# A decoder step with product-key retrieval: the normed rows h2 move from SBUF into two banks of PSUM, and the two score components take turns in the other two

## The chip, the cores and the metric

The kernel runs on one core of one Trainium2 chip. The metric is the device time of one execution in microseconds (us), the median over several runs. Lower is better.

## The reference, cut to what matters

One layer of a decoder: norm, one input projection, differential attention (4 heads, two components a head) beside a pooling mixer, one output projection, a residual, and then PEER: each token picks 16 experts for each of 8 heads out of 16,384, takes the dot of its normed row with each expert's row of `w_u`, and adds up the experts' rows of `w_v`, weighted by the gelu of the dot and a gate. 1,040 prompt rows (16 of them meta tokens) and 32 sample rows go through it.

```python
def diff_attn(q, k, v, q_pos, k_pos, lam):
    s = jnp.einsum('bqhcd,bkhcd->bchqk', q, k) * (QK_DIM ** -0.5)
    s = jnp.where(k_pos[None, :] <= q_pos[:, None], s, NEG)
    p = jax.nn.softmax(s, axis=-1)
    a = p[:, 0] - lam * p[:, 1]
    return jnp.einsum('bhqk,bkhd->bqhd', a, v)

def peer(xb, w_query, sub_keys, w_u, w_v):            # xb: 128 normed rows (h2)
    s = jnp.einsum('thcd,hcnd->thcn', (xb @ w_query).reshape(...), sub_keys)
    sv, si = lax.top_k(s, 16)
    ...                                               # 16 x 16 candidates, top 16 of them
    gate = jax.nn.softmax(top, axis=-1)
    a = jnp.einsum('td,thkd->thk', xb, w_u[eidx])     # 128 dots a row, each over 1024
    a = jax.nn.gelu(a, approximate=False) * gate
    return jnp.einsum('thk,thkd->td', a, w_v[eidx])
```

## The kernel before, in words

The rows are cut into 9 tiles of 128 (tile 8 holds the last 16 prompt rows and the 32 sample rows). A head part projects all tiles; then the product of query weights and sub-keys is folded into one routing weight; then tile 0 runs its attention, routing and choice of experts alone. From there on the kernel goes in turns: turn t gathers tile t's experts while tile t+1 goes through attention, projection, routing and choice. There are 8 turns of 128 steps and a last one of 64 steps (tile 8 is folded in two halves).

A step k of a turn is one pick of all 128 rows. GpSimd (POOL) issues two indirect gathers, 128 rows of 4 KB each: the `w_u` rows (`gather_u`, L541) and, one step behind, the `w_v` rows (`gather_v`, L548). Both read their row numbers from `idx_c` in SBUF. VectorE (DVE) takes the dot of the `w_u` rows with `h2c` (`g_step`, L1416), ScalarE (ACT) makes gelu, amplitude and a diagonal matrix of it (L987, L999, L1003), and TensorE (PE) multiplies that diagonal with the `w_v` rows and accumulates in Y (L823). There are 5 slots of rows: a `w_u` row's slot is free after the gelu of its dot (`u_free`), a `w_v` row's slot after its matmuls (`v_free`).

Each engine runs its own program in a fixed order: step k of the retrieval, then what the class `Plan` puts at step k for the next tile (`a_part`). Head h of the attention starts at step 1 + 9h, and `Plan` gives offsets from there: the score matmuls (`scores_of`, L649; component c in bank pair S0 or S1, at most 512 keys a matmul), the scaling and masking on DVE with the row minimum (`scale_mask`, L1142), the exponentials on ACT (`exps`, L902), the combination of both components on DVE (`combine`, L1170 and L1175), the transposes on PE (`flip`, L677), their evacuation on ACT (`evac`, L914) and the product with the values on PE (`values`, L690). Tile t has min(t+1, 8) x 128 keys, tile 8 another 48. Projection, routing (`route`, L777, four banks of 512 columns, taken out by ACT at L973) and the choice of experts (`top_part`, DVE) follow in steps 49 to 121. At a turn's end `promote` writes h2 of the next tile into `h2c` (L1405).

Semaphores tie the engines together. Those that the change touches: `s_free` (a score bank is free again), `s_ready` (scores are there), `nm_ready` (minimum is there), `exp_ready`, `a_used` (the previous head's matrix has been transposed, its buffer may be written), `t_free` (bank T is free).

PSUM has 8 banks of 512 columns: Y and S0 and S1 two each, T and O one each.

Of the kernel before, what the change touches and what calls it, by code (L numbers as in the profile page):

```python
# [28 lines left out]
ALU = mybir.AluOpType  # L29
# [3 lines left out]
P = 128  # L33
# [60 lines left out]
class Plan:  # L94
# [3 lines left out]
    scores, scale, exp = (0, 1, 2, 3), (4, 5), (5, 6)  # L98
# [46 lines left out]
def build(nc, x, xT, g1T, w_in, gqk, cs, mt, mst, state, w_pool, b_poolT, scaleT, wqT, skT, g2T, g2b, lams,  # L145
          rows01, w_out, subT, mask, mext, msam, ktc, vc, pages, wu, wv, iota,
          y_all, k_all, v_all, p_last, state_old):
    with ExitStack() as ctx:
# [116 lines left out]
        S = [S0, S1]  # L265
# [5 lines left out]
        route_bank = [S0[:, 0:512], S0[:, 512:1024], S1[:, 0:512], S1[:, 512:1024]]  # L271
# [64 lines left out]
        route_ready, sc_ready = sem("route_ready"), sem("sc_ready")  # L336
        gexp_in, gexp_out = sem("gexp_in"), sem("gexp_out")
# [223 lines left out]
        def _(pe):  # L561
# [76 lines left out]
            def scores_of(h, u, t):  # L638

                c, m = divmod(u, 2)  # L640
                r = slice(QK * c, QK * c + QK)
                if h == 0 and u == 0:
                    pe.wait_ge(qp_in, n(qp_in, 16))
                if u == 0:
                    pe.wait_ge(s_free, n(s_free))
                w = keys_of(t)
                lo, hi = m * 512, min((m + 1) * 512, w)
                if lo < w:
                    mm = pe.matmul(bank_of(c, t)[:, lo:hi], qT[r, h, :], KT3[r, h, lo:hi], start=True, stop=True)  # L649
                    if hi == w and t < LAST:  # L650
                        mm.then_inc(s_ready, 1)
                if u == 3 and t == LAST:

                    pe.wait_ge(t_free, n(t_free))
                    for c in range(2):
# [190 lines left out]
        def _(act):  # L846
# [51 lines left out]
            def exps(c, t):  # L898
# [9 lines left out]
                if c == 1:  # L908
                    act.sem_inc(exp_ready, 1)
# [9 lines left out]
            def a_part(k, t):  # L919
                at = Plan  # L920
                for h in range(HEADS):
                    for c in at.head(k, at.exp, h):
                        exps(c, t)
# [93 lines left out]
        def _(dve):  # L1017
# [114 lines left out]
            def scale_mask(h, c, t):  # L1132

                last = t == LAST
                if c == 0:
                    if h == 0:
                        dve.wait_ge(mask_in, n(mask_in, 16))
                    else:
                        dve.wait_ge(a_used, n(a_used))
# [5 lines left out]
                if last:  # L1145
                    dve.tensor_tensor_reduce(out=[ex0, ex1][c], in0=T[:, c * ROWS8:(c + 1) * ROWS8], in1=emask[:, :],
                                             scale=-(QK ** -0.5), scalar=3e38, op0=ALU.add, op1=ALU.min,
                                             accum_out=nmx[:, 2 + c:3 + c]).then_inc(dve_own, 1)
                    dve.wait_ge(dve_own, n(dve_own, 2))
                    dve.tensor_tensor(nm[:, c:c + 1], nmx[:, c:c + 1], nmx[:, 2 + c:3 + c], ALU.min).then_inc(dve_own, 1)  # L1150
# [244 lines left out]
            def promote(t, last=False):  # L1395
# [9 lines left out]
                dve.scalar_tensor_tensor(h2c[:, :], x1n, r2, g2w[:, :], ALU.mult, ALU.mult).then_inc(dve_own, 1)  # L1405
                dve.wait_ge(dve_own, n(dve_own))
                if last:
                    dve.tensor_copy(h2c[FOLD:ROWSF, :], h2c[0:ROWS8, :]).then_inc(dve_own, 1)
# [3 lines left out]
            def g_step(t, k):  # L1412
# [3 lines left out]
                dot = dve.tensor_tensor_reduce(out=ring[s][:, 0:D], in0=ring[s][:, 0:D], in1=h2c[:, :],  # L1416
# [187 lines left out]
```

## Time and profile before

| what | value |
|---|---|
| median of 3 runs | 3609.66 us (3595.9 to 3618.48) |
| the profiled execution's own time | 3600.91 us |
| its span, first to last instruction | 3598.9 us |
| mean granted TensorE clock | 0.96 |
| PE / DVE / ACT / POOL busy | 3062.0 / 2194.4 / 1421.2 / 2340.0 us |
| DMA | 1216.25 MB, mean 338 GB/s over the span |

Busy time is an average over a head part of some 440 us, in which POOL and the gathers do nothing, and over the turns. So the page's shares are read only to find the engines that matter; the turns are read one by one from windows of the trace, and within a turn the heads, the routing and the choice apart. A row of a window gives the stretch and its length, then for PE, PEld (TensorE's weight loads), DVE, ACT and POOL the busy time and in brackets the count of instructions, then the granted clock, the DMA engines' busy share and GB/s. A row of a timeline gives start, length, engine, line and operation, and in square brackets how long the engine was idle before it and who ended that. A row of a group gives the count, the busy time, the mean of one in ns, and behind the second bar the idle time before its instructions and who ended it.

### The profile page before, as it was taken

What the parts mean: (1) busy time and instruction counts of PE and PEld (TensorE: products, weight loads), DVE (VectorE), ACT (ScalarE), POOL (GpSimd) and SP (SyncE); (2) the same over time, 40 slices, a digit from 0 to 9 for tenths busy, and PEclk for the clock granted to TensorE, in tenths of its full rate; (3) what the DMA queues carried; (4) which work ended last, traced back from release to release, by engine and by line L of the source; (5) the groups of instructions that cost most, each with busy time, mean ns of one, the idle gap of its engine ahead of it and who ended that gap; (6) DMA issues with size and microseconds to landing.
All of it is one profiled execution on the core that took longest, in us unless ns stands there. A gap on an engine that the chain in (4) does not pass through costs nothing.

```text
span 3598.9 us, 32093 instructions
## 1 busy us (share of the span) xinstructions
PE 3062.0 (85%) x7658; PEld 1317.5 (37%) x7658; DVE 2194.4 (61%) x5098; ACT 1421.2 (39%) x3898; POOL 2340.0 (65%) x2195
## 2 busy tenths in 40 slices
PE   7999777897889789978897999788979897889877
PEld 3446453342334233323332433243324342343311
DVE  2224455588558755975497549754975487446944
ACT  1221105433643454345434543454345433543333
POOL 0000007777777777777777777777776777567776
PEclk9999879999999999999999999999999999999999
DMA  5224229999999999999999999999999999899999
GB/s 200 82 88 176 62 82 375 407 373 392 385 402 376 390 391 395 382 390 366 389 385 394 369 384 382 382 350 377 390 389 338 371 380 387 277 336 377 384 392 371
DMA packets 342466, 1216.25 MB, mean 338 GB/s; under 512 B 39641, under 2 KB 40025, under 8 KB 342153
## 3 DMA queue, kind: packets, MB, share of 16 engines
q0 software_dynamic: 313344, 1140.99, 82.8%
q1 hardware_dynamic: 28944, 73.30, 5.8%
q8 instruction: 62, 1.02, 0.1%
q14 instruction: 116, 0.94, 0.1%
HBM read 1200.28 MB, written 14.04 MB: 337 GB/s over the span
## 4 chain that ended last, share of the span: by engine, by line
POOL 33%; PE 29%; DVE 15%; issue 12%; ACT 7%; DMA 4%; DVEq 0%; ACTq 0%; SPq 0%; POOLq 0%; PEldq 0%
POOL big L548 13%; POOL big L541 13%; PE Y L823 12%; DVE big L1416 5%; POOL slot L541 3%; PE Y L581 3%; POOL slot L548 3%; PE S L581 3%; PE S L757 2%; DMA slot<-in_wv,idx_c 2%; DVE qpw L1252 2%; ACT L987 2%; PE S L649 2%; PE Y L739 1%; DVE qpw L1249 1%
## 5 line engine op out<-in xcount | busy, mean ns | idle before, releaser
L823 PE MATMUL Y<-big,diag 128*128 128x512 f32 (+1 forms) x3540 | 1759.7, 625 | 387.7 <-ACT diag L1003 258.6
L1416 DVE CUSTOM_DVE_ANT_0 big<-big,h2c 128x1024 f32<-128x1024 f32 x885 | 1081.2, 1229 | 603.8 <-DMA big<-in_wu,idx_c 574.0
L541 POOL DMA_INDIRECT big<-in_wu,idx_c x885 | 926.9, 1047 | 583.1 <-issue 266.0
L823 PEld LDWEIGHTS Y<-big,diag 128*128 128x128 f32 (+1 forms) x3540 | 633.4, 191 | 1381.4 <-issue 949.5
L548 POOL DMA_INDIRECT big<-in_wv,idx_c x885 | 948.0, 1071 | 274.0 <-issue 264.4
L987 ACT ACTIVATE gel<-dots 128x1 f32<-128x1 f32 x1088 | 219.2, 201 | 1295.4 <-DVE dots L1416 1243.0
L823 PE MATMUL Y<-slot,diag 128*128 128x512 f32 (+1 forms) x812 | 403.5, 620 | 70.1 <-ACT diag L1003 42.2
L1003 ACT ACTIVATE diag<-ident,amp 128x128 f32<-128x128 f32 x1024 | 411.2, 402 | 33.9
L999 ACT ACTIVATE amp<-gel,gate_c 128x1 f32<-128x1 f32 x1088 | 320.6, 295 | 130.5 <-ACT gel L987 3.6
L1416 DVE CUSTOM_DVE_ANT_0 slot<-slot,h2c 128x1024 f32<-128x1024 f32 x203 | 249.5, 1229 | 161.5 <-DMA slot<-in_wu,idx_c 154.6
L777 PE MATMUL S<-big,work 128*128 128x512 f32 x576 | 293.9, 598 | 0.8 <-issue 0.8
L541 POOL DMA_INDIRECT slot<-in_wu,idx_c x203 | 223.1, 1099 | 77.5 <-issue 60.0
L548 POOL DMA_INDIRECT slot<-in_wv,idx_c x203 | 223.1, 1099 | 63.7 <-issue 61.0
L823 PEld LDWEIGHTS Y<-slot,diag 128*128 128x128 f32 (+1 forms) x812 | 143.8, 191 | 289.0 <-issue 193.3
L520 POOL TENSOR_TENSOR big<-big 128x1024 f32<-128x1024 f32 x9 | 17.1, 1898 | 247.2 <-DMA big<-in_xT 247.2
L777 PEld LDWEIGHTS S<-big,work 128*128 128x128 f32 x576 | 109.5, 192 | 135.5 <-issue 135.0
L1249 DVE MAX8 qpw<-work 128x8 f32<-128x128 f32 (+1 forms) x432 | 126.6, 327 | 46.9 <-ACTq L976 38.3
L1252 DVE FIND_INDEX8 qpw<-qpw,work 128x8 uint32<-128x128 f32 (+1 forms) x432 | 138.0, 330 | 0.0
L1142 DVE CUSTOM_DVE_ANT_0 work<-S,maskw 128x1024 f32<-128x1024 f32 (+7 forms) x72 | 58.1, 807 | 103.6 <-ACTq L934 44.2
L987 ACT ACT_TABLE_LOAD x89 | 114.2, 1283 | 10.6 <-DVE dots L1416 6.7
L581 PE MATMUL Y<-big 128*128 128x512 f32 x256 | 113.2, 601 | 4.7 <-issue 4.7
L581 PE MATMUL S<-big 128*128 128x512 f32 x256 | 111.2, 592 | 0.0
(181 smaller groups left out, 2113.6 us busy)
## 6 DMA issues: line engine op xcount, KB each, us to landing
big<-in_wu,idx_c POOLq DMA_INDIRECT x885, 6.3
big<-in_wv,idx_c POOLq DMA_INDIRECT x885, 6.4
big<-in_w_in SPq DMA_DIRECT2D x8, 1024.0 KB, 11.3
big<-in_wqT SPq DMA_DIRECT2D x4, 2048.0 KB, 7.6
big<-in_xT SPq DMA_DIRECT2D x9, 512.0 KB, 3.8
big<-in_x SPq DMA_DIRECT2D x9, 512.0 KB, 4.6
big<-in_mt SPq DMA_DIRECT2D x9, 512.0 KB, 5.2
qp_dram<-big SPq DMA_DIRECT2D x9, 512.0 KB
```

The lines of the kernel that those rows point to most:

```text
L541: pool.indirect_dma_start(ring[s][:, 0:D], None, wu, bass.IndirectOffsetOnAxis(ap=idx_c[:, k:k + 1], axis=0)).then_inc(u_landed[s], 16)
L548: pool.indirect_dma_start(ring[s][:, D:2 * D], None, wv, bass.IndirectOffsetOnAxis(ap=idx_c[:, k:k + 1], axis=0)).then_inc(v_landed[s], 16)
L581: mm = pe.matmul(zbank[q], hxT[par][:, c * P:(c + 1) * P], w_in_sb[:, q, c, :], start=(c == 0), stop=(c == DC - 1))
L649: mm = pe.matmul(bank_of(c, t)[:, lo:hi], qT[r, h, :], KT3[r, h, lo:hi], start=True, stop=True)
L777: mm = pe.matmul(route_bank[q], aT[:, c * P:(c + 1) * P], w_route[:, c, q * 512:(q + 1) * 512], start=(c == 0), stop=(c == DC - 1), skip_g ...
L823: mm = pe.matmul(Y[0:w, m * 512:(m + 1) * 512], diag[:, s * P:s * P + w], ring[s][:, D + m * 512:D + (m + 1) * 512], start=(k == 0), stop= ...
L987: act.activation(gel[:, s:s + 1], dots[:, s:s + 1], ACT.Gelu).then_inc(act_own, 1)
L999: act.activation(amp[:, s:s + 1], gel[:, s:s + 1], ACT.Copy, scale=gate_c[:, k:k + 1])\
L1003: act.activation(diag[:, s * P:s * P + w], (ident if w == P else fold_id)[:, 0:w], ACT.Copy, scale=amp[:, s:s + 1]).then_inc(diag_ready, 1)
L1249: dve.max(values[:, g, lo:lo + 8], source[:, g, :]).then_inc(dve_own, 1)
L1252: dve.max_index(indices[:, g, lo:lo + 8], values[:, g, lo:lo + 8], source[:, g, :])\
L1416: dot = dve.tensor_tensor_reduce(out=ring[s][:, 0:D], in0=ring[s][:, 0:D], in1=h2c[:, :], scale=1.0, scalar=0.0, op0=ALU.mult, op1=ALU.add ...
```

## The change

The normed rows stand in S1 (now called H) and no longer in `h2c`; the dot's first operand is H in PSUM, its second the gathered rows in SBUF. With S1 taken, the scores of both components use S0, one after the other, component 1 first; a component's matmuls wait until the other's scores have been scaled out of the bank. In `Plan` the score matmuls move from offsets 0, 1, 2, 3 to 0, 1, 3, 4, the scalings from 4, 5 to 2, 5, the exponentials from 5, 6 to 3, 6 (both at 6 for tile 8). The wait for `a_used` goes from the first scaling of a head to the second. Routing uses the two banks of S0 in turn, with a new semaphore `route_free`. For tile 8 the 48 extra keys of both components are scored and scaled together with the second component.

```diff
-    scores, scale, exp = (0, 1, 2, 3), (4, 5), (5, 6)
+    scores, scale, exp, exp_last = (0, 1, 3, 4), (2, 5), (3, 6), (6, 6)
...
-        S = [S0, S1]
+        H = S1
...
-        route_bank = [S0[:, 0:512], S0[:, 512:1024], S1[:, 0:512], S1[:, 512:1024]]
+        route_bank = [S0[:, 0:512], S0[:, 512:1024]]
...
         def bank_of(c, t):
-            return S0[:, 512 * c:512 * c + P] if t == 0 else S[c][:, 0:keys_of(t)]
+            return S0[:, 512 * c:512 * c + P] if t == 0 else S0[:, 0:keys_of(t)]
...
             def scores_of(h, u, t):
-                c, m = divmod(u, 2)
+                turn, m = divmod(u, 2)
+                c = 1 - turn
...
-                if u == 0:
+                if m == 0 and (turn == 0 or t > 0):
                     pe.wait_ge(s_free, n(s_free))
...
-                    if hi == w and t < LAST:
+                    if hi == w and (t < LAST or turn == 0):
                         mm.then_inc(s_ready, 1)
...
-                    pe.sem_inc(s_ready, 2)
+                    pe.sem_inc(s_ready, 1)
...
-                mm = pe.matmul(route_bank[q], aT[:, c * P:(c + 1) * P], w_route[:, c, q * 512:(q + 1) * 512],
+                if c == 0 and q >= 2:
+                    pe.wait_ge(route_free, n(route_free))
+                mm = pe.matmul(route_bank[q % 2], aT[:, c * P:(c + 1) * P], w_route[:, c, q * 512:(q + 1) * 512],
...
-                    for c in at.head(k, at.exp, h):
-                        exps(c, t)
+                    for turn in at.head(k, at.exp if t < LAST else at.exp_last, h):
+                        exps(1 - turn, t)
...
             def scale_mask(h, c, t):
-                if c == 0:
-                    if h == 0:
-                        dve.wait_ge(mask_in, n(mask_in, 16))
-                    else:
-                        dve.wait_ge(a_used, n(a_used))
+                if c == 1 and h == 0:
+                    dve.wait_ge(mask_in, n(mask_in, 16))
+                if c == 0 and h > 0:
+                    dve.wait_ge(a_used, n(a_used))
                 dve.wait_ge(s_ready, n(s_ready))
...
-                if c == 1:
+                if c == 0 or t > 0:
                     dve.sem_inc(s_free, 1)
...
-                dve.scalar_tensor_tensor(h2c[:, :], x1n, r2, g2w[:, :], ALU.mult, ALU.mult).then_inc(dve_own, 1)
+                dve.scalar_tensor_tensor(H[:, :], x1n, r2, g2w[:, :], ALU.mult, ALU.mult).then_inc(dve_own, 1)
...
-                dot = dve.tensor_tensor_reduce(out=ring[s][:, 0:D], in0=ring[s][:, 0:D], in1=h2c[:, :],
+                dot = dve.tensor_tensor_reduce(out=ring[s][:, 0:D], in0=H[:, :], in1=ring[s][:, 0:D],
```

DVE in turn 4, the second head of tile 5 (768 keys), before: `big1` and `slot5` are the slots of gathered rows, the rows with `dots` alone read the sum out, and the rows on S0 and S1 are the two scalings.

```order
L1416 ISA big1,dots<-big1,h2c 128x1024 [waits u_landed2]
L1416 ISA dots 128x1
L1416 ISA big1,dots<-big1,h2c 128x1024 [waits u_landed3]
L1416 ISA dots 128x1
L1416 ISA slot5,dots<-slot5,h2c 128x1024 [waits u_landed4]
L1416 ISA dots 128x1
L1142 ISA work,sm<-S0,maskw 128x768 [waits s_ready,a_used]
L1142 ISA sm 128x1
L1416 ISA big1,dots<-big1,h2c 128x1024 [waits dve_own,u_landed0]
L1416 ISA dots 128x1
L1142 ISA work,sm<-S1,maskw 128x768 [waits s_ready]
L1142 ISA sm 128x1
```

The same steps of DVE now.

```order
L1425 ISA big1,dots<-S1,big1 128x1024 [waits u_landed2]
L1425 ISA dots 128x1
L1148 ISA work,sm<-S0,maskw 128x768 [waits s_ready]
L1148 ISA sm 128x1
L1425 ISA big1,dots<-S1,big1 128x1024 [waits dve_own,u_landed3]
L1425 ISA dots 128x1
L1425 ISA slot5,dots<-S1,slot5 128x1024 [waits u_landed4]
L1425 ISA dots 128x1
L1425 ISA big1,dots<-S1,big1 128x1024 [waits u_landed0]
L1425 ISA dots 128x1
L1148 ISA work,sm<-S0,maskw 128x768 [waits s_ready,a_used]
L1148 ISA sm 128x1
```

The first scaling stands two dots earlier, without the wait for `a_used`; the second stands where it stood and has taken that wait over.

PE in the same head, before: three steps with the second component's matmuls (L649 on S1) behind steps of offset 2 and 3; L677 are transposes and L690 values of the head before.

```order
L823 MATMUL Y<-big1,diag 128x512 [waits diag_ready,v_landed2]
L823 MATMUL Y<-big1,diag 128x512
L677 MATMUL T<-ident,work 128x128 [waits t_free]
L677 MATMUL T<-ident,work 128x128
L649 MATMUL S1<-KT,qpw 128x512
L823 MATMUL Y<-big1,diag 128x512 [waits diag_ready,v_landed3]
L823 MATMUL Y<-big1,diag 128x512
L690 MATMUL O<-V,work 128x128 [waits o_free,t_evac]
L690 MATMUL O<-V,work 128x128
L649 MATMUL S1<-KT,qpw 128x256
```

And now, from the step of offset 3 on.

```order
L828 MATMUL Y<-big1,diag 128x512 [waits diag_ready,v_landed3]
L828 MATMUL Y<-big1,diag 128x512
L693 MATMUL O<-V,work 128x128 [waits o_free,t_evac]
L693 MATMUL O<-V,work 128x128
L652 MATMUL S0<-KT,qpw 128x512 [waits s_free]
L828 MATMUL Y<-slot5,diag 128x512 [waits diag_ready,v_landed4]
L828 MATMUL Y<-slot5,diag 128x512
L693 MATMUL O<-V,work 128x128 x2
L652 MATMUL S0<-KT,qpw 128x256
```

The second component's last scores now come behind the step of offset 4, the scaling that needs them is still that of offset 5, and their first matmul waits for `s_free`.

## Rows read from the trace of the kernel before

**Rows 1.** The page, part 4: the chain that ended last, by engine.

```profile
POOL 33%; PE 29%; DVE 15%; issue 12%; ACT 7%; DMA 4%; DVEq 0%; ACTq 0%; SPq 0%; POOLq 0%; PEldq 0%
```

**Rows 2.** Windows, turns 0-8, turn 7's heads: PE, PEld, DVE, ACT, POOL, clock, DMA.

```profile
443.80:877.60 433.80, 356.79 (x966) 167.41 (x966) 285.61 (x775) 157.84 (x441) 267.71 (x255) 0.93 0.84 320
877.60:1229.10 351.50, 300.77 (x677) 122.79 (x678) 235.40 (x553) 157.96 (x443) 270.83 (x257) 0.97 1.00 389
1229.10:1579.40 350.30, 302.02 (x692) 122.81 (x690) 236.76 (x550) 158.26 (x440) 270.59 (x257) 0.98 1.00 389
1579.40:1935.30 355.90, 307.02 (x713) 128.65 (x714) 239.72 (x551) 160.20 (x444) 276.89 (x257) 0.97 1.00 383
1935.30:2292.60 357.30, 310.83 (x732) 127.84 (x730) 240.90 (x550) 161.49 (x444) 274.01 (x256) 0.98 0.99 382
2292.60:2656.00 363.40, 315.45 (x737) 131.80 (x738) 243.10 (x551) 162.69 (x444) 277.23 (x256) 0.96 0.99 375
2656.00:3026.00 370.00, 318.35 (x756) 132.28 (x754) 244.84 (x550) 164.06 (x444) 278.43 (x256) 0.98 0.98 369
3026.00:3416.80 390.80, 331.66 (x777) 139.91 (x778) 249.05 (x589) 166.98 (x464) 274.82 (x257) 0.94 0.93 349
3416.80:3586.50 169.70, 127.18 (x263) 28.96 (x262) 81.57 (x131) 53.71 (x194) 130.67 (x129) 0.98 1.01 397
3038.40:3170.30 131.90, 108.26 (x273) 46.40 (x273) 64.80 (x139) 67.55 (x161) 73.20 (x71) 0.91 0.84 300
```

**Rows 3.** One line's instructions, L548: duration in ns, min/median/max.

```profile
L548 POOL DMA_INDIRECT big<-in_wv,idx_c x885: 932/939/1983, 446.5 to 3585.5; - x177
```

**Rows 4.** Timeline of POOL and DVE, turn 2: start, length, what, idle before.

```profile
1510.21 1.22 DVE L1416 CUSTOM_DVE_ANT_0 big<-big,h2c 128x1024 f32<-128x1024 f32 x1
1510.93 1.31 POOL L548 DMA_INDIRECT slot<-in_wv,idx_c  x1 [0.31 <-issue]
```

**Rows 5.** Timeline of POOL and DVE, a scaling in turn 6.

```profile
2765.17 1.23 DVE L1142 CUSTOM_DVE_ANT_0 work<-S,maskw 128x1024 f32<-128x1024 f32 x1 [5.43 <-ACTq L934]
2765.82 0.94 POOL L541 DMA_INDIRECT big<-in_wu,idx_c  x1 [0.30 <-ACTq L989]
2766.59 1.23 DVE L1416 CUSTOM_DVE_ANT_0 big<-big,h2c 128x1024 f32<-128x1024 f32 x1 [0.19 <-DVE sm L1142]
```

**Rows 6.** Groups by form, DVE: the dot, and the scaling at 1024 columns.

```profile
L1416 DVE CUSTOM_DVE_ANT_0 big<-big,h2c 128x1024 f32<-128x1024 f32 x885 | 1081.2, 1229 | 603.8 <-DMA big<-in_wu,idx_c 574.0 <-DVE sm L1142 5.3 <-DVE work L1355 3.0
L1142 DVE CUSTOM_DVE_ANT_0 work<-S,maskw 128x1024 f32<-128x1024 f32 x16 | 19.6, 1223 | 55.6 <-PEq L660 35.1 <-ACTq L934 16.5 <-PE S L649 4.0
```

**Rows 7.** Windows: two stretches of turn 3, and the choice of experts in turn 1.

```profile
1722.00:1762.00 40.00, 38.50 (x91) 16.70 (x92) 19.66 (x35) 16.55 (x51) 30.54 (x32) 1.00 1.03 410
1622.00:1662.00 40.00, 38.29 (x108) 17.29 (x108) 22.29 (x40) 23.02 (x54) 31.90 (x27) 1.00 0.98 360
1163.60:1217.00 53.40, 41.56 (x83) 14.99 (x82) 51.51 (x147) 18.21 (x60) 41.51 (x40) 0.94 1.00 387
```

**Rows 8.** Timeline of PE and ACT in the first head of turn 3 (tile 4, 640 keys).

```profile
1600.85 0.48 PE L649 MATMUL S<-KT,qpw 64*128 64x128 f32 x2
1601.27 1.98 PE L823 MATMUL Y<-big,diag 128*128 128x512 f32 x4
1603.18 1.12 PE L649 MATMUL S<-KT,qpw 64*128 64x512 f32 x2
...
1606.46 0.40 ACT L1003 ACTIVATE diag<-ident,amp 128x128 f32<-128x128 f32 x1
...
1610.75 0.20 ACT L987 ACTIVATE gel<-dots 128x1 f32<-128x1 f32 x1
...
1611.40 0.40 ACT L1003 ACTIVATE diag<-ident,amp 128x128 f32<-128x128 f32 x1
```

**Rows 9.** Groups, PE: the values' matmuls (count, busy us, mean ns, idle before).

```profile
L690 PE MATMUL O<-V,work 128*128 128x128 f32 x352 | 57.8, 284 | 2.4 <-ACTq L917 2.4
```

**Rows 10.** The page, part 6: a gather's us from issue to landing.

```profile
big<-in_wv,idx_c POOLq DMA_INDIRECT x885, 6.4
```

More of the change, by code:

```diff
@@ L336, in build @@
         route_ready, sc_ready = sem("route_ready"), sem("sc_ready")
+        route_free = sem("route_free")
         gexp_in, gexp_out = sem("gexp_in"), sem("gexp_out")
@@ L654, in scores_of @@
                     pe.wait_ge(t_free, n(t_free))
-                    for c in range(2):
+                    for c in (1, 0):
                         r = slice(QK * c, QK * c + QK)
@@ L907, in exps @@
                 act.wait_ge(act_own, n(act_own, 2 if last else 1))
-                if c == 1:
+                if c == 0:
                     act.sem_inc(exp_ready, 1)
@@ L972, in a_part @@
                         act.wait_ge(route_ready, n(route_ready))
-                        act.activation(work[:, q * 512:(q + 1) * 512], route_bank[q], ACT.Copy, scale=r2)\
+                        act.activation(work[:, q * 512:(q + 1) * 512], route_bank[q % 2], ACT.Copy, scale=r2)\
                             .then_inc(act_own, 1)
@@ L976, in a_part @@
                         act.sem_inc(sc_ready, 1)
+                        if q < 2:
+                            act.sem_inc(route_free, 1)
                         if q == 3:
@@ L1144, in scale_mask @@
                                          accum_out=low[:, c:c + 1]).then_inc(dve_own, 1)
[L1145 to L1150, printed above, removed]
-                dve.wait_ge(dve_own, n(dve_own))
-                dve.sem_inc(nm_ready, 1)
-                if c == 1:
+                if last and c == 0:
+                    for x in range(2):
+                        dve.tensor_tensor_reduce(out=[ex0, ex1][x], in0=T[:, x * ROWS8:(x + 1) * ROWS8],
+                                                 in1=emask[:, :], scale=-(QK ** -0.5), scalar=3e38, op0=ALU.add,
+                                                 op1=ALU.min, accum_out=nmx[:, 2 + x:3 + x]).then_inc(dve_own, 1)
+                    dve.wait_ge(dve_own, n(dve_own, 3))
+                    dve.tensor_tensor(nm[:, 0:2], nmx[:, 0:2], nmx[:, 2:4], ALU.min).then_inc(dve_own, 1)
+                dve.wait_ge(dve_own, n(dve_own))
+                if not last:
+                    dve.sem_inc(nm_ready, 1)
+                if last and c == 0:
+                    dve.sem_inc(nm_ready, 2)
+                    dve.sem_inc(t_free, 1)
+                if c == 0 or t > 0:
                     dve.sem_inc(s_free, 1)
-                    if last:
-                        dve.sem_inc(t_free, 1)
             def combine(part, t):
@@ L1321, in a_part @@
                 for h in range(HEADS):
-                    for c in at.head(k, at.scale, h):
-                        scale_mask(h, c, t)
+                    for turn in at.head(k, at.scale, h):
+                        scale_mask(h, 1 - turn, t)
                     for part in at.head(k, at.combine, h):
@@ L1404, in promote @@
                     dve.sem_inc(idx_hi, 1)
[L1405 removed]
+                dve.scalar_tensor_tensor(H[:, :], x1n, r2, g2w[:, :], ALU.mult, ALU.mult).then_inc(dve_own, 1)
                 dve.wait_ge(dve_own, n(dve_own))
                 if last:
[L1408 removed]
+                    dve.tensor_copy(H[FOLD:ROWSF, :], H[0:ROWS8, :]).then_inc(dve_own, 1)
                     dve.wait_ge(dve_own, n(dve_own))
```

## The prediction

> **What bounds the kernel now.** I read the page's chain first, then the turns one by one, then the engines in one turn. The chain runs through POOL for a third of the span [rows 1], though POOL does nothing here but issue gathers. By windows, turns 1 and 2 take 351 us each, and the later ones grow to 391 with the number of keys [rows 2]. In turn 1 POOL is busy 270.83 us over 257 gathers, 1.054 us each, and 0.30 us lies ahead of each [rows 4]: 256 x 1.359 = 348 us of 351.5. So POOL issues without a break, and its issuing is the length of the turn. But a gather's median is 0.939 us and the longest took 1.98 [rows 3]. The timeline shows what stretches one: a gather that starts 0.72 us after a dot takes 1.31 us and ends behind the dot [rows 4], while one that starts 0.65 us after a scaling of the same length takes 0.94 [rows 5]. The dot reads two operands from SBUF, the scaling one from PSUM and one from SBUF. Over all turns POOL is busy 2321 us for 2180 counted gathers; at 0.939 that would be 2047 [rows 2, 3]: some 274 us are gathers held behind DVE.
>
> What lies next behind POOL? Undisturbed, two gathers a step are 2 x (0.939 + 0.305) = 2.49 us, 318 a turn. The DMA share is 1.00 in turns 1 to 3 [rows 2], but that is no limit yet: in a stretch of turn 3 without held gathers 410 GB/s pass at the share 1.03, in one with held gathers 360 at 0.98 [rows 7]. At 410 a step's 1.049 MB take 2.557 us. So the DMA engines end a step 0.07 us later than a free POOL would. A third limit is local: in the 20 steps of the choice of experts DVE is busy 51.5 of 53.4 us, 2.67 a step [rows 7].
>
> **The change part by part.** *Dots.* 1088 dots read PSUM in place of SBUF; no instruction is added. Their duration is that of the scaling, the same operation with one PSUM and one SBUF operand at 1024 columns: 1223 ns against 1229 [rows 6]. I take 0 (6 ns a dot at most, under 7 us, on either side). The Trainium skill (VectorE: DVE Perf Modes, "The TRN2 errata") speaks against it: 120 cycles fixed with a PSUM source, 58 from SBUF, an estimated 65 ns more a dot and 10 us more in the stretches where DVE is the bound. The two measured means differ the other way, so the measurement decides.
>
> *Gathers.* With one SBUF operand the dots hold none [rows 5]. A turn without trouble is then 108 steps x 2.557 = 276.2, 20 steps x 2.67 = 53.4 (there DVE stays the bound), and the tile's own loads and stores, 1.8 MB by the code, 4.5 us at 410 GB/s: 334.1 us. The few other DVE instructions with two SBUF operands still hold gathers, which the 0.07 us a step between POOL and DMA covers (9 us a turn).
>
> *Attention.* This is the price. A step's dot runs early on DVE and its matmuls late on PE, behind diagonal and landing. Before, the scalings at offsets 4 and 5 needed scores of PE's steps 1 and 3; now those at 2 and 5 need steps 1 and 4, one step back. Behind the waiting scaling stand DVE's next dots, behind those ACT's gelus and the freeing of slots. Up to 512 keys (turns 0 to 2) the scores end in steps 0 and 3, two steps back. For more keys I add up the loop for 640 keys, from the end of the first scores: scaling to dot 1.0 (1.42 at 1024 columns, less 384 columns at 1.2 ns) [rows 5, 6], dot and hand-over 1.3, gelu to diagonal 1.05, exponential with its table loads to the next diagonal 4.94 (1606.86 to 1611.80) [rows 8], PE's step 4 with 1.9, two value matmuls of 0.16 and the last scores 0.4 [rows 8, 9], together 2.7 with the hand-over: the second scores end at 11.0. Again 8.3 to the diagonal of step 7: 19.3. Then PE's steps 7 to 10, 4 x 1.9, with 1.05 and 0.4 of the next head's scores and 0.65 of transposes (at the price of rows 9): 29.1 us for a loop of 9 steps that DMA would do in 23.0. The same sum at 512 keys, where PE's steps 4 and 10 and the first exponential drop out of the loop: 0.9 + 1.3 + 1.05, PE's step 3 with its scores 3.4, 0.9 + 1.3 + 1.05 + 4.9, PE's steps 7 to 9 with scores 6.9: 21.7, under 23.0, so no loss in turns 0 to 2. Beyond 640, each 128 keys more add about 0.9 (2 x 0.15 scaling, 2 x 0.21 scores, 2 x 0.1 exponential, the last an estimate from its share of the 4.94). The slots cover a delay: 5 steps, 12.8, less 6.4 from issue to landing [rows 10], less 1.9 of matmuls, leave 4.5 us once a turn. Three loops pass between the first and the last head, and behind the last PE reaches its step 7 at 19.3 where 12.4 would be on time, 7.0 late. So turn 3 loses 3 x 6.1 + 7.0 - 4.5 = 20.8 us, turns 4, 5 and 6 23.9, 27.4 and 30.5. Turns 3 to 6 come to 354.9, 358.0, 361.5 and 364.6: 1439.0 against 1446.6 [rows 2].
> The ends of this unknown: no loss (the loop hides in the slots) and tile 8's price. Tile 8 already has the one-step distance before the change: 35.1 us of waits for L660 in four heads, 8.8 each [rows 6], and 131.9 us for 36 steps of heads [rows 2], 40 more than DMA needs. My value lies between, nearer to the upper row, because tile 8 also has its extra keys.
>
> *Tile 8 (turn 7).* It exchanges one such distance for another and saves two table loads a head; its heads stay at 132 (2 us more). The other 92 steps go from 258.9 to 334.1 - 92.1 = 242: 15 us gained.
>
> *Routing* in two banks: ACT takes a quarter out one step after it is ready, PE wants the bank back 8 steps later. 0. *Writing h2*, 9 times 1024 columns, and the part before the turns: 0, within 3 us.
>
> **The sum**, against the profiled execution's 3600.9 us (2 us over its span, 9 under the median shown). Turn 0: issuing took 267.71 + 255 x 0.305 = 345.5, becomes 334.1: -11.4. Turns 1, 2: -33.6. Turns 3 to 6: -7.6. Turn 7: -15. Turn 8: 64 steps at 2.557 and 2 us of stores, 166 for 169.7: -3.5. Together -71: 3530 us, 2.0% less. DMA is the new bound in turns 0 to 2, the loop PE, DVE, ACT in the heads of turns 3 to 7.
>
> **Rivals.** *The head waits are hidden* (A). The second scaling no longer waits 5.4 us alone for the evacuation [rows 5], and exponentials two steps further apart leave PE shorter gaps. Then turns 3 to 6 are 334.1 each, 110 us less than now: 3427. Against it: tile 8.
> *The gathers are not relieved* (B): the dots hold them still, or DMA is full anyway; for it speaks the share of 1.00 [rows 2]. Turns 0 to 2, 7 and 8 stay, turns 3 to 6 start from 351 at 2.74 a step and lose 13.8, 17, 20 and 24 by the same loop: +32, 3633. Against it: rows 5 and the 410 GB/s of rows 7. The Trainium skill (SBUF — State Buffer, "Who interferes with whom") has both sides: an instruction with two SBUF inputs contends with a GpSimd instruction that reads SBUF, yet such an instruction was not seen to stall a DMA, as generating descriptors is inferred to need the write side only. By the second sentence this change gains nothing; in this trace the gathers, which read their row numbers from SBUF, are held (rows 4), so the first one holds.
> *Every head pays tile 8's price* (C, the slower side): DVE's wait for scores one step back throws PE late, which makes the next head's scores late, and two steps are too few as well. At 131.9 for 36 steps, turns 0 to 6 are 374 each: +28 for turn 0, +46 for turns 1 and 2, +50 for 3 to 6, -18 for 7 and 8: 3707. It decides from an average of 25 us lost in the heads of turns 0 to 6 (all other gains, 174, over 7); I forecast 0 in three and 26 in four. Against it: the 21.7 us at 512 keys.
>
> **How the numbers follow.** Forecast 0.60 (its own range 3485 to 3580: 8 us more or less a turn in the heads, 4 in the base), A 0.17, B 0.12, C 0.11. A measurement here tells about 1% from no change: 3565 to 3637. Below: A and 0.52 of the forecast's 0.60, 0.69. Within: the other 0.08, B and C's mildest forms, 0.21. Above: the rest of C, 0.10. For 8 in 10 the range goes from A's price to just short of B's: 3430 to 3610.
>
> **What would show it.** Dots' mean within 10 ns of 1229; gathers' mean at 0.95 and POOL busy near 2070 in the turns: the first step right. Gathers still at 1.05: B. Turns 1 and 2 at 334 and some 405 GB/s: the DMA bound right. Waits of the scalings for PE's score line, about two a head and several us each, in turns 3 to 6 alone, and windows of 355 to 365 there: the loop right; 335 there means A, turns 0 to 2 above 350 with waits at small tiles means C. The dots in the choice of experts much longer than 1.23 would break the first step.

## The result, and the profile after

The changed kernel takes 3656.67 us (median of 4 runs, 3648.74 to 3656.82), the kernel before, timed beside it, 3602.86 us (3595.9 to 3618.48). The ratio is 1.014, with a 95% interval of 1.011 to 1.017: slower by 1.4%. The prediction said 3530 us, faster, with 3610 as the upper end of its range. It was wrong in its sign.

Half of the mechanism came as forecast. The first fence is the group of the page that holds the dots; the second is one line's instructions, `gather_v` (now L549): duration in ns, min/median/max. Both are of the changed kernel.

```profile
L1425 DVE CUSTOM_DVE_ANT_0 big<-S,big 128x1024 f32<-128x1024 f32 x885 | 1072.6, 1224 | 470.3 <-DMA big<-in_wu,idx_c 435.8
L549 POOL DMA_INDIRECT big<-in_wv,idx_c x885 | 845.1, 955 | 291.4 <-issue 242.8
```

```profile
L549 POOL DMA_INDIRECT big<-in_wv,idx_c x885: 935/941/1705, 450.2 to 3640.3; - x177
```

A dot from PSUM takes 1224 ns against 1229 [rows 6], and the gathers' mean is 0.955 us with the median where it was [rows 3]: hardly one is held. The page's chain shows what that did to POOL: 9% where 33% stood [rows 1], and PE and DVE have its place.

```profile
PE 36%; DVE 31%; POOL 9%; ACT 9%; issue 8%; DMA 7%; DVEq 0%; ACTq 0%; SPq 0%; POOLq 0%; PEldq 0%
```

The windows of the turns, with the columns of [rows 2], show where the time went. Here are turns 0, 1, 3 and 7 of the changed kernel, then the heads (steps 1 to 37) of turns 1 and 5, and last the 44 steps of the choice of experts (77 to 121) in turn 1.

```profile
447.60:876.30 428.70, 359.27 (x963) 169.59 (x964) 286.22 (x775) 156.70 (x440) 243.15 (x256) 0.91 0.85 324
876.30:1222.70 346.40, 301.13 (x679) 121.22 (x678) 237.19 (x553) 157.49 (x442) 243.72 (x257) 0.98 1.01 394
1566.80:1939.00 372.20, 313.65 (x718) 130.91 (x719) 239.72 (x553) 159.87 (x448) 242.98 (x257) 0.95 0.97 367
3083.90:3475.30 391.40, 327.96 (x782) 138.38 (x783) 249.49 (x587) 156.60 (x460) 246.12 (x256) 0.95 0.93 350
890.60:983.20 92.60, 80.06 (x190) 31.48 (x191) 52.98 (x103) 59.31 (x143) 67.10 (x72) 1.00 1.03 410
2330.80:2459.80 129.00, 98.57 (x239) 42.03 (x239) 58.59 (x104) 61.82 (x140) 65.52 (x70) 0.93 0.85 304
1087.70:1213.70 126.00, 109.31 (x237) 42.98 (x235) 116.83 (x337) 41.30 (x133) 87.33 (x91) 0.98 1.00 385
```

POOL is busy 243 to 246 us a turn where it was 268 to 278 [rows 2], and yet turn 1 is only 5 us shorter (351.5 before), and turn 3 is 16 us longer (355.9 before). Turns 0 to 2 gained 5, 5 and 6 us, turns 3 to 6 lost 16, 20, 20 and 14, turn 7 lost 1, and turn 8 gained 4: with 4 us lost before the first turn and 1 behind the last, that is the 56 us between the two profiled executions. The last rows say why in both cases. In turn 1's heads the DMA engines run at the 410 GB/s of [rows 7], 92.6 us for 36 steps that take 92.1 at 2.557: there the gathers are free and the time is DMA's. In the choice DVE is busy 116.8 of 126.0 us, whatever POOL does. In turn 5's heads 36 steps take 129 us, and DMA has a share of 0.85: no engine there works without pause.

What the heads wait for stands in the view of the scaling's line (L1148): how long DVE sat idle before it, and until what.

```profile
  PE S L652: 296.2, 63
  PEq L663: 27.7, 4
```

L652 is the score matmul, L663 the step of PE that holds tile 8's extra keys. The same lines of the kernel before, where the scores are L649, the extra keys L660, and L934 is where ACT, behind its evacuation, lets the matrix's buffer be written again:

```profile
  ACTq L934: 44.2, 15
  PEq L660: 35.1, 4
  PE S L649: 23.0, 19
```

So 23 us of waits for the scores became 296, at 63 of the 72 scalings. The wait for L934 is gone; all waits of the scalings together went from 103 us to 325.

### The profile page after: what moved, and what is told of

Its sections match the earlier page's. It is cut to its first block, busy times and chain, and to the rows that moved or that the text cites. A ratio compares the mean times of both kernels' runs of the same rounds, so it can differ in the third digit from the quotient of the medians.

```text
span 3654.5 us, 32127 instructions
## 1 busy us (share of the span) xinstructions
PE 3078.3 (84%) x7658; PEld 1328.2 (36%) x7658; DVE 2195.5 (60%) x5094; ACT 1405.4 (38%) x3890; POOL 2091.9 (57%) x2195
## 4 chain that ended last, share of the span: by engine, by line
PE 36%; DVE 31%; POOL 9%; ACT 9%; issue 8%; DMA 7%; DVEq 0%; ACTq 0%; SPq 0%; POOLq 0%; PEldq 0%
PE Y L828 18%; DVE big L1425 10%; DVE qpw L1261 4%; POOL big L542 4%; POOL big L549 4%; DMA big<-in_wv,idx_c 3%; PE S L760 3%; PE Y L582 3%; PE S L582 3%; DMA slot<-in_wv,idx_c 3%; DVE qpw L1258 3%; DVE slot L1425 2%; PE S L782 2%; DVE work L1267 2%; ACT L994 2%
## 5 line engine op out<-in xcount | busy, mean ns | idle before, releaser
L828 PE MATMUL Y<-big,diag 128*128 128x512 f32 (+1 forms) x3540 | 1774.2, 629 | 409.6 <-ACT diag L1010 315.3
L1425 DVE CUSTOM_DVE_ANT_0 big<-S,big 128x1024 f32<-128x1024 f32 x885 | 1072.6, 1224 | 470.3 <-DMA big<-in_wu,idx_c 435.8
L542 POOL DMA_INDIRECT big<-in_wu,idx_c x885 | 839.9, 949 | 797.2 <-ACTq L996 289.1
L828 PEld LDWEIGHTS Y<-big,diag 128*128 128x128 f32 (+1 forms) x3540 | 640.4, 193 | 1407.3 <-issue 1092.6
L549 POOL DMA_INDIRECT big<-in_wv,idx_c x885 | 845.1, 955 | 291.4 <-issue 242.8
L828 PE MATMUL Y<-slot,diag 128*128 128x512 f32 (+1 forms) x812 | 406.2, 624 | 84.7 <-ACT diag L1010 67.4
L1425 DVE CUSTOM_DVE_ANT_0 slot<-S,slot 128x1024 f32<-128x1024 f32 x203 | 248.4, 1224 | 116.6 <-DMA slot<-in_wu,idx_c 107.5
L542 POOL DMA_INDIRECT slot<-in_wu,idx_c x203 | 194.7, 959 | 148.0 <-ACTq L996 91.9
L828 PEld LDWEIGHTS Y<-slot,diag 128*128 128x128 f32 (+1 forms) x812 | 145.5, 192 | 309.1 <-issue 247.7
L1148 DVE CUSTOM_DVE_ANT_0 work<-S,maskw 128x1024 f32<-128x1024 f32 (+7 forms) x72 | 58.3, 810 | 325.4 <-PE S L652 296.2
L549 POOL DMA_INDIRECT slot<-in_wv,idx_c x203 | 193.2, 952 | 64.7 <-issue 59.1
```

What stands on the lines that cost most here:

```text
L542: pool.indirect_dma_start(ring[s][:, 0:D], None, wu, bass.IndirectOffsetOnAxis(ap=idx_c[:, k:k + 1], axis=0)).then_inc(u_landed[s], 16)
L549: pool.indirect_dma_start(ring[s][:, D:2 * D], None, wv, bass.IndirectOffsetOnAxis(ap=idx_c[:, k:k + 1], axis=0)).then_inc(v_landed[s], 16)
L828: mm = pe.matmul(Y[0:w, m * 512:(m + 1) * 512], diag[:, s * P:s * P + w], ring[s][:, D + m * 512:D + (m + 1) * 512], start=(k == 0), stop= ...
L1425: dot = dve.tensor_tensor_reduce(out=ring[s][:, 0:D], in0=H[:, :], in1=ring[s][:, 0:D], scale=1.0, scalar=0.0, op0=ALU.mult, op1=ALU.add, ...
```

## The experiments

Each kernel is the changed one with the edit shown. The turns below are windows from the first `w_u` gather of a turn to that of the next, in us, of each kernel's profiled execution.

| kernel | 0 | 1 | 2 | 3 | 4 | 5 | 6 | 7 | median, us |
|---|---|---|---|---|---|---|---|---|---|
| before | 433.8 | 351.5 | 350.3 | 355.9 | 357.4 | 363.4 | 370.0 | 390.7 | 3602.9 |
| changed | 428.7 | 346.4 | 344.2 | 372.2 | 377.6 | 383.5 | 383.9 | 391.4 | 3656.7 |
| scores together | 428.3 | 346.2 | 344.6 | 348.2 | 345.0 | 352.0 | 351.5 | 370.3 | 3520.7 |
| exponentials together | 430.2 | 344.7 | 346.1 | 365.5 | 370.0 | 377.5 | 380.1 | 391.5 | 3643.0 |
| both together | 428.2 | 346.9 | 347.6 | 347.2 | 353.1 | 356.5 | 359.7 | 370.8 | 3541.7 |
| first only | 428.6 | 346.2 | 344.5 | 358.5 | 365.3 | 375.7 | 376.4 | 384.8 | 3609.5 |
| second only | 429.7 | 345.3 | 345.8 | 353.4 | 352.2 | 361.6 | 364.9 | 382.7 | 3563.8 |
| scores late | 447.3 | 361.8 | 364.9 | 375.1 | 381.3 | 380.3 | 385.9 | 390.9 | 3720.2 |
| dots from SBUF | 435.8 | 352.7 | 351.0 | 372.8 | 389.0 | 386.6 | 392.9 | 393.9 | 3704.8 |
| SBUF, scores together | 436.4 | 349.0 | 357.0 | 355.5 | 351.9 | 359.3 | 365.2 | 377.4 | 3583.2 |
| lighter choice | 422.8 | 337.3 | 339.2 | 336.8 | 338.1 | 346.0 | 348.3 | 368.1 | 3461.6 |
| second sooner | 431.0 | 345.7 | 346.3 | 344.0 | 345.5 | 348.1 | 349.5 | 363.3 | 3498.0 |
| choice later | 430.4 | 346.0 | 345.2 | 344.7 | 345.0 | 351.2 | 352.7 | 371.7 | 3513.4 |
| second sooner, choice later | 426.6 | 345.0 | 344.2 | 346.9 | 342.9 | 349.6 | 347.2 | 361.7 | 3486.9 |

**Scores together.** Both halves of a component's scores move into one step of PE. Nothing else changes: the bank pair is shared, the scalings stay at 2 and 5.

```diff
-    scores, scale, exp, exp_last = (0, 1, 3, 4), (2, 5), (3, 6), (6, 6)
+    scores, scale, exp, exp_last = (0, 0, 3, 3), (2, 5), (3, 6), (6, 6)
```

> The changed kernel with both halves of a component's scores in one step of PE (offsets 0, 0, 3, 3 for 0, 1, 3, 4); nothing else moves, the components still share one bank pair. Theory 1 (the scalings come one step of the retrieval too soon behind the scores): for 640 keys and more the scores now end two steps ahead of the scaling, as they do at up to 512 keys, so turns 3 to 6 fall from 372-384 us to 350-357 and turn 7 from 391 to about 360: 3525 to 3560 us. Theory 2 (the shared bank itself: scores, scaling, scores, scaling in a chain, however they are spaced): 3640 to 3660, as the changed kernel. Theory 3 (the exponentials' table loads between the steps make PE late): 3640 to 3660.

Measured: 3520.66 us, ratio to before 0.978 (0.976 to 0.980). One digit in two places takes 136 us off, 3.7% of the changed kernel, and the kernel is now faster than before. Theory 1 holds (4 us below its range); theories 2 and 3 had no gain here. The scaling's waits and turn 5's heads in this kernel:

```profile
  PE S L652: 133.2, 63
  PEq L663: 18.0, 4
```

```profile
2271.40:2369.30 97.90, 88.44 (x237) 40.33 (x238) 59.15 (x103) 62.12 (x140) 65.07 (x70) 0.97 0.99 383
```

The heads take 97.9 us for 129.0, and DMA is back at a share of 0.99.

**Exponentials together.**

```diff
-    scores, scale, exp, exp_last = (0, 1, 3, 4), (2, 5), (3, 6), (6, 6)
+    scores, scale, exp, exp_last = (0, 1, 3, 4), (2, 5), (6, 6), (6, 6)
```

> The changed kernel with both exponentials of a head at offset 6 in every tile, as tile 8 has it (one pair of table loads a head less, and no exponential between the first scaling and the second scores). Theory 1: the one-step distance stays, the loop gets shorter by one pair of loads, some 2.6 us a head in turns 3 to 6: 16 x 2.6 = 40 us less, 3600 to 3635. Theory 2: 3640 to 3660. Theory 3: turns 3 to 6 fall to about 350, turn 7 stays at 391, because it has both exponentials together already: 3540 to 3570.

Measured: 3642.99 us, ratio 1.012 (1.010 to 1.014). Theory 3 falls: turns 3 to 6 get only 4 to 8 us shorter. Theory 1's 40 us was too much as well: 14 us came. The time lies in theory 2's range, but scores together has ruled theory 2 out.

**Both together.**

> Both edits: scores at 0, 0, 3, 3 and both exponentials at offset 6. Theory 1: turns 3 to 7 at 348 to 355, 3510 to 3550. Theory 2: 3600 to 3650. Theory 3: no better than the exponentials alone.

Measured: 3541.65 us, ratio 0.984 (0.982 to 0.986), inside what theory 1 said, but 21 us over the scores alone. So with the distances right it is better to leave the exponentials apart. That one long stop of ACT a head delays more than two shorter ones is a possible reading, but was not tried by itself.

**First only, second only.** One component's scores in one step, the other's as in the changed kernel; the first line that is added is first only's, the second one second only's.

```diff
-    scores, scale, exp, exp_last = (0, 1, 3, 4), (2, 5), (3, 6), (6, 6)
+    scores, scale, exp, exp_last = (0, 0, 3, 4), (2, 5), (3, 6), (6, 6)
+    scores, scale, exp, exp_last = (0, 1, 3, 3), (2, 5), (3, 6), (6, 6)
```

> The changed kernel with only the first component's scores in one step (offsets 0, 0, 3, 4): the first scaling of a head is two steps behind its scores, the second stays one step behind. Theory 1a (both one-step distances stand in one loop of PE, DVE and ACT a head, and share its loss): about half of the 136 us between the changed kernel and the one with both in one step, turns 3 to 6 at 358 to 368, 3575 to 3605 us. Theory 1b (the second distance alone makes the loss): 3635 to 3660. Theory 1c (the first alone): 3520 to 3540.

> The same with only the second component's scores in one step (offsets 0, 1, 3, 3). Theory 1a: 3575 to 3605. Theory 1b: 3520 to 3540. Theory 1c: 3635 to 3660.

Measured: 3609.5 us (ratio 1.002, 1.001 to 1.004) and 3563.8 us (0.989, 0.986 to 0.993). Both are a little outside 1a's "about half": the first distance is worth 47 us, the second 93. Together that is 140, and both at once gave 136. So each distance costs for itself, and the two costs add up; neither 1b nor 1c holds. Why the second costs twice the first was not tried apart.

**Scores late.** The suspected cost is given to the small tiles, which the change had spared.

```diff
-    scores, scale, exp, exp_last = (0, 1, 3, 4), (2, 5), (3, 6), (6, 6)
+    scores, scale, exp, exp_last = (1, 1, 4, 4), (2, 5), (3, 6), (6, 6)
```

> The changed kernel with both halves of the scores one step later than in the kernel with them together (offsets 1, 1, 4, 4): now the scores end one step ahead of the scaling at every number of keys, so the small tiles get the distance that only the tiles of 640 keys and more have in the changed kernel. Theory 1 (the distance makes the loss): turns 0 to 2 get 13 to 24 us longer (turn 3's loss of 26, less 4 to 5 us for each 128 keys fewer), turns 3 to 7 stay as in the changed kernel: 3700 to 3730 us. Theory k (the number of keys makes it, by longer scalings and a second matmul of scores, and the distance matters little): turns 0 to 2 stay at 429, 346 and 344: 3645 to 3665.

Measured: 3720.15 us, ratio 1.035 (1.032 to 1.039). Turns 0 to 2 go from 429, 346 and 344 to 447, 362 and 365, turns 3 to 7 stay within 4 us. The number of keys is not the cause: 256 keys pay too, as soon as their scores end one step ahead of the scaling.

**Dots from SBUF.** The attention as changed, the dots as before.

```diff
-                dve.scalar_tensor_tensor(H[:, :], x1n, r2, g2w[:, :], ALU.mult, ALU.mult).then_inc(dve_own, 1)
+                dve.scalar_tensor_tensor(h2c[:, :], x1n, r2, g2w[:, :], ALU.mult, ALU.mult).then_inc(dve_own, 1)
...
-                dot = dve.tensor_tensor_reduce(out=ring[s][:, 0:D], in0=H[:, :], in1=ring[s][:, 0:D],
+                dot = dve.tensor_tensor_reduce(out=ring[s][:, 0:D], in0=ring[s][:, 0:D], in1=h2c[:, :],
```

> The changed kernel with the attention as changed, but the dots multiply with the normed rows in SBUF as before (S1 is written by nobody in the turns). It prices the attention part alone. Gathers should be held again (mean near 1.05 us in turns 0 to 2). Theory a (what freed gathers bring is nearly all covered, by DVE in the 44 steps of the choice and by the head waits): 5 us more in each of turns 0 to 2, nothing to 3 us in the others, 3665 to 3690. Theory b (freed gathers are worth the 17 us a turn that was forecast, and the whole miss lies in the heads): 3740 to 3790.

Measured: 3704.76 us, ratio 1.028 (1.026 to 1.030), between both theories. Attention and routing as changed cost 102 us against before, the freed gathers give 48 back. The group of `gather_v` in this kernel shows that it is the operand's place that holds a gather:

```profile
L549 POOL DMA_INDIRECT big<-in_wv,idx_c x885 | 939.4, 1061 | 275.3 <-issue 264.7 <-PE Y L828 10.7
```

**SBUF, scores together.** Both edits. It is the fourth corner.

> Scores at 0, 0, 3, 3 and the dots with the normed rows in SBUF: shared bank and two-step distance, without the freed gathers. With the three others it gives the four corners of dots in PSUM or SBUF by one or two steps. Theory a (freed gathers are worth 5 to 7 us a turn in turns 0 to 2, and more in the later turns, since the heads no longer end last): 3580 to 3610, about the kernel before. Theory b (the freed gathers are worth the 48 us seen with one-step distances, whatever the distance): 3560 to 3575. If the shared bank costs something by itself that the distance does not, it is over 3610.

Measured: 3583.23 us, ratio 0.994 (0.992 to 0.996). By the corners, PSUM dots are worth 48 us at one-step distances (3704.8 to 3656.7) and 63 us at two steps (3583.2 to 3520.7); theory a's range holds the result. Theory b's 48 at any distance is unlikely: its range ends 8 us below the median, and 2 of the 10 runs lie in it. The shared bank itself costs nothing that shows: with dots from SBUF and two-step distances the kernel is 20 us under the one before, which had two bank pairs.

**Lighter choice.** On top of scores together (its line is not repeated), `top16` leaves out the replacing of the eight largest values, so the search for ranks 9 to 16 repeats ranks 1 to 8.

```diff
-                if lo == 0:
-
-                    for g in which:
-                        dve.match_replace(source[:, g, :], values[:, g, lo:lo + 8], source[:, g, :], -3e38)\
-                            .then_inc(dve_own, 1)
-                    dve.wait_ge(dve_own, n(dve_own, m))
```

> Scores at 0, 0, 3, 3 and the choice of experts without the replacing of the eight largest values (24 instructions of 0.41 us on DVE in a tile, 9.8 us): left out is the search for ranks 9 to 16, which repeats ranks 1 to 8. Theory c (DVE is the bound in all 44 steps of the choice, 77 to 121, at 2.75 us a step, not in 20 steps as the prediction had it): the three quarters behind the first fall from 2.75 us a step to 2.56, the turns get 8 to 10 us shorter, tile 0's own choice too, 3435 to 3455 us. Theory d (PE, 0.96 busy in the routing steps, or the DMA engines hold these steps): 1 to 3 us a turn and tile 0's 10, 3490 to 3505.

Measured: 3461.6 us, ratio 0.960 (0.957 to 0.963), 59 us under scores together: nearer to c, short of its range. The 44 steps of the choice in turn 1, first of scores together, then of this kernel:

```profile
1084.80:1210.40 125.60, 109.84 (x237) 43.45 (x235) 116.50 (x337) 41.30 (x133) 87.17 (x91) 0.97 1.00 383
```

```profile
1079.10:1196.50 117.40, 105.58 (x237) 43.15 (x235) 107.17 (x287) 41.07 (x133) 87.20 (x91) 1.00 1.02 404
```

DVE's busy time falls by 9.3 us and the stretch by 8.2; DMA rises to 404 GB/s. The last three quarters of the choice now run at 2.50 to 2.65 us a step for 2.73 to 2.76 (from the starts of the dots). DVE was the bound there, and DMA, just behind it, is next. The rows gathered are other ones, but turn 1's heads take 91.4 us for 92.0, so easier gathers are not the reason. Turns 1 and 2 come to 337 and 339 us, near the 334 that the prediction gave them. In the profiled executions, 50 us apart, turns 1 and 3 gain 9 and 11 us, about what c gave to every turn; turns 0, 2, 4 and 5 gain 5 to 7, turns 6 and 7 only 2 to 3, and the part before the turns 0.4. There the sum stays short of c.

**Second sooner.** The second component's scores one step earlier, so that three steps lie before their scaling. The edit is shown against scores together; tile 8's third transpose goes one step ahead with it, so that bank T is free for its extra scores.

```diff
-    scores, scale, exp, exp_last = (0, 0, 3, 3), (2, 5), (3, 6), (6, 6)
-    combine, flip, evac, values = (8, 9), (10, 11, 12), (11, 12, 12), (12, 13, 14, 15)
+    scores, scale, exp, exp_last = (0, 0, 2, 2), (2, 5), (3, 6), (6, 6)
+    combine, flip, evac, values = (8, 9), (10, 11, 11), (11, 12, 12), (12, 13, 14, 15)
```

> Scores at 0, 0, 2, 2 (and tile 8's third transpose one step sooner, offset 11, so that bank T is free for its extra scores): the second scaling stands three steps behind its scores, the first two. Theory 1, continued (the waits that are left at 640 keys and more, 153 us over all scalings where the changed kernel has 325, are mostly those for the second scores, which counted double): turns 5 and 6 fall from 352 to 345-348, turn 7 from 370 to 358-365: 3495 to 3512. If the waits left are the first scaling's, 3515 to 3530.

Measured: 3497.99 us, ratio 0.972 (0.969 to 0.976), as expected. The scalings' waits are down to half of what scores together had left:

```profile
  PE S L652: 67.5, 37
  PEq L663: 10.6, 4
```

**Choice later**, once on top of scores together and once on top of second sooner.

```diff
-    top, tops = take[0] + 1, 44
+    top, tops = take[0] + 3, 42
```

> Scores at 0, 0, 3, 3 and the choice of experts two steps later (steps 79 to 121, 42 steps for 44). At its start DVE sits idle 4.3 us for the first quarter of the routing scores, in a stretch in which DVE is the bound. If that idle time is lost for good, the dots of two more steps fill it: 4 us a turn in 8 turns less, 3485 to 3500. If the dots get late by the same amount either way: 3513 to 3528.

> Both of the edits before: scores at 0, 0, 2, 2 and the choice from step 79. If both hold, 3465 to 3490; each alone as above.

Measured: 3513.37 us (0.978, 0.974 to 0.981) and 3486.90 us (0.970, 0.966 to 0.973). The turns of the first do not get shorter. In the 44 steps of turn 1 DVE no longer waits 4.8 us for the routing scores, but it now waits 4.9 us, in five waits, for gathered rows: 125.7 us for 125.6. The second is the fastest kernel of the study, 3.0% under before, but its interval overlaps that of second sooner alone (0.969 to 0.976).

## Why the prediction was wrong

**Dots and gathers: right.** The dots' price of 0 came out as 5 ns less a dot, the gathers' mean as 0.955 us for "0.95", POOL's busy time in the turns as 2072.8 us for "near 2070". The Trainium skill (VectorE: DVE Perf Modes, "The TRN2 errata") would have had each dot longer from PSUM; this trace, 1224 for 1229 ns, does not agree. Of the two sentences of the Trainium skill (SBUF — State Buffer, "Who interferes with whom") that the prediction sets side by side, the first is borne out: gathers are held when the dot takes both operands from SBUF (mean 1061 ns in the kernel with dots from SBUF) and hardly otherwise (955).

**The undisturbed turn: the first wrong term.** The base of every turn, 334.1 us, had 108 steps at 2.557, 20 at 2.67 and 4.5 us of loads and stores; turns 1 and 2 took 346.4 and 344.2. The 20 steps were wrong. The third row of [rows 7] was read as the choice of experts, but it is its last part: the choice starts at step 77, beside the routing matmuls. For 44 steps the prediction's prices are 24 x 2.557 + 20 x 2.67 = 114.8 us; the row above has 126.0 with DVE busy 116.8, and with the gathers held the kernel before took 124.8 for the same steps of turn 1. The 11.2 us between 114.8 and 126.0 are the whole error of a turn (the mean of turns 1 and 2, 345.3, less 334.1). They are of two kinds, as the first 11 of these steps, the other 33, and DVE's one long wait show:

```profile
1087.70:1122.80 35.10, 34.05 (x79) 14.32 (x77) 29.13 (x83) 10.37 (x32) 24.25 (x25) 1.00 1.01 391
1122.80:1213.70 90.90, 75.26 (x159) 28.66 (x158) 87.69 (x255) 30.94 (x101) 63.08 (x66) 0.97 1.00 383
1093.84 0.49 DVE L1258 MAX8 qpw<-work 128x8 f32<-128x128 f32 x2 [4.88 <-ACTq L981]
```

The 33 steps take 90.9 us for 86.6: DVE works in all of them, 2.75 us a step, and is never idle for more than 0.04 us. The 11 steps take 35.1 us for 28.1: there DVE waits 4.9 us until ACT has taken the first quarter of the routing scores out, a wait that the prediction does not have. What would hold these steps without it is open, since choice later moved the wait and gained nothing. So freeing POOL bought 5 us a turn and not 17: in 44 of 128 steps POOL had not been the bound. The lighter choice shows it, since it takes DVE's time there away and gets 337 and 339 us. Over turns 1 to 6 the term is 67 us short, in turn 0 6 us, and in turn 7 11 of 15. With it alone put right the sum would have been about 3614 us, already above the 3601 of the kernel before.

**The loop in the heads: the right mechanism, too small.** The prediction had the scaling wait one step behind its scores at 640 keys and more, and no loss at 512 and fewer: scores together and scores late show both, and the waits are as described, two a head of 4.4 to 9.9 us each in turns 3 to 6, none over 2.1 us in turns 1 and 2. Its losses for turns 3 to 6 were 20.8, 23.9, 27.4 and 30.5 us. Measured over the 345.3 of turns 1 and 2 they are 27, 32, 38 and 39: 33 us more in all. The timeline of turn 5 (896 keys) shows the term that was too small. It runs from a first scaling to the second one, PE, ACT and DVE, parts left out:

```profile
2339.20 1.09 DVE L1148 CUSTOM_DVE_ANT_0 work<-S,maskw 128x896 f32<-128x896 f32 x1 [4.86 <-PE S L652]
...
2340.58 1.23 DVE L1425 CUSTOM_DVE_ANT_0 slot<-S,slot 128x1024 f32<-128x1024 f32 x1 [0.28 <-DVE sm L1148]
...
2341.84 0.20 ACT L994 ACTIVATE gel<-dots 128x1 f32<-128x1 f32 x1 [6.42 <-DVE dots L1425]
...
2342.49 0.40 ACT L1010 ACTIVATE diag<-ident,amp 128x128 f32<-128x128 f32 x1
...
2342.91 1.28 ACT L907 ACT_TABLE_LOAD   x1
2343.04 1.95 PE L828 MATMUL Y<-slot,diag 128*128 128x512 f32 x4 [2.08 <-ACT diag L1010]
...
2347.30 0.40 ACT L1010 ACTIVATE diag<-ident,amp 128x128 f32<-128x128 f32 x1
...
2347.84 3.34 PE L828 MATMUL Y<-big,diag 128*128 128x512 f32 x4 [1.80 <-ACT diag L1010]
...
2351.11 1.17 PE L652 MATMUL S<-KT,qpw 64*128 64x384 f32 x2
...
2352.33 1.09 DVE L1148 CUSTOM_DVE_ANT_0 work<-S,maskw 128x896 f32<-128x896 f32 x1 [8.23 <-PE S L652]
```

Scaling to dot 1.38, dot to gelu 1.26, gelu to diagonal 1.05, from there to the next diagonal 4.81: these are near the prediction's terms for this tile (1.3, 1.3, 1.05 and 5.1). But PE's step 4 takes 3.34 us where the sum had 1.9. PE sat idle ahead of that step, and its granted clock in such a step is near the lower of its two levels (1.2 of 2.4 GHz):

```profile
2356.50:2358.50 2.00, 1.96 (x4) 0.67 (x4) 1.09 (x2) 1.99 (x2) 1.23 (x2) 1.00 0.50 86
2358.50:2361.40 2.90, 0.00 (x0) 0.01 (x1) 2.39 (x6) 2.60 (x7) 0.66 (x1) 1.00 0.78 291
2361.40:2364.70 3.30, 3.28 (x5) 1.51 (x6) 3.11 (x4) 2.26 (x8) 2.37 (x3) 0.58 0.67 180
```

These are three windows in the other half of the same loop: a step at 1.00 in 1.96 us, 2.9 us in which PE does nothing, and a step at 0.58 in 3.3 us. In this turn such a step costs 1.3 to 1.6 us more, but not every half of a head has one. The three loops of turn 3, each from one head's first scaling to the next head's, show what it does. In these rows PE and PEld are the retrieval's matmuls (L828) alone:

```profile
1589.24:1620.67 31.43, 20.44 (x37) 7.23 (x37) 0.89 0.91 337
1620.67:1649.70 29.03, 17.20 (x37) 6.26 (x38) 1.00 0.87 303
1649.70:1682.10 32.40, 20.19 (x37) 7.10 (x37) 0.89 0.87 327
```

The loop without a slow step takes 29.0 us, and the sum had 29.1; the two others, at a granted clock of 0.89, spend 3 us more on the same 37 matmuls and are 2.4 and 3.4 us longer. In all twelve loops of turns 3 to 6 the steps below full clock are over 1.95 us by 26 us together, and the loops are over the sum (29.1, and 0.9 more for each 128 keys) by 24, most of the 33. In turn 5's heads the same 140 matmuls take 75.1 us in the changed kernel and 68.2 with the scores together, of PE's 98.6 and 88.4 us:

```profile
2330.80:2459.80 129.00, 75.09 (x140) 26.52 (x140) 0.93 0.85 304
2271.40:2369.30 97.90, 68.23 (x140) 25.48 (x140) 0.97 0.99 383
```

So the term that failed here is the 1.9 us for each of PE's steps in the loop. That was read from the traces; no run changed the clock alone.

**Tile 8 and routing: nearly right.** Turn 7's heads take 134.3 us where the sum had 134 (132 and 2 more); its other 92 steps take 257.1 us for 242. Of these 15 us 11 are the base term again and 4 lie in steps 37 to 77 (108.2 us for 104.5 in turn 1). Turn 8 took 165.9 us for 166. Routing in two banks left 1.9 us of waits for a bank in the whole run.

**The rivals.** A (hidden) and B (gathers not relieved) are out. C had the right sign for a reason that does not hold here: not every head pays, only those with 640 keys and more. What decided between the forecast and the slower side was the sum of small terms. 67 us too little in the base of turns 1 to 6, 33 in the loops, 16 and 6 in turns 7 and 0, and 4 at the start and the end make the 127 us, but for rounding. The prediction had given the slower side 0.10, on the argument that only a loss in all heads could bring it.

## What to carry to other kernels

In programs that each run in a fixed order, look how many steps lie between a producer and its consumer on another engine, and how late the producer runs behind: here one step cost up to 33 us a turn (turn 4, 377.6 us for 345.0), and with the same work two steps ahead turns 3 to 6 lie within 7 us of turns 1 and 2. Price every stretch of a loop by its own bound before crediting a freed engine with the whole loop, and find the stretch's borders in the program and not in a convenient window. When an edit frees a resource and loses time elsewhere, time the four corners: the loss here was a matter of two offsets, and the gain was worth 63 us once they were right.

## What was not expected of the hardware

TensorE's granted clock falls within a head: after 2.9 us in which PE did nothing, the next step ran at 0.58 and its four matmuls took 3.3 us for 1.96. In the same head, a step after 2.1 us of idle time ran at full speed (1.95 us), and one after 1.8 us did not (3.34 us), so the idle time directly before does not tell it. A wait on PE's path can therefore cost more than its length.

Two exponentials in one step save a pair of table loads of 1.28 us each (124 loads in the run for 180), and yet the kernel with them and the scores together is 21 us slower than with the scores alone.

Freed gathers also cost DVE something. One of its small casts in the choice of experts, here before and after, min/median/max in ns, takes 0.42 us where it took 0.18, and 0.18 again with the dots from SBUF:

```profile
L1316 DVE CAST idx_n<-maskw x36: 180/181/182, 443.1 to 3405.1; 128x32 int32<-128x32 f32 x36
L1325 DVE CAST idx_n<-maskw x36: 180/424/429, 446.8 to 3464.6; 128x32 int32<-128x32 f32 x36
```

It goes with the gathers that are no longer held; the reason was not tried apart. It is small, but there DVE is the bound: a step of the last three quarters of the choice takes 2.75 us for 2.73 before.
